# Two-layer transformer kernel: four blocks end, and three begin, by token tile over four steps

## The chip, the cores and the metric

The kernel runs on 1 core of one Trainium2 chip. The metric is device time in microseconds (us), the lower the better. TensorE (PE in the profile) multiplies, VectorE (DVE), ScalarE (ACT) and GpSimd (POOL) do the rest, and SyncE (SP) issues the transfers.

## What is computed

A first transformer layer (sliding-window attention beside a state-space mixer, then a gated MLP) is followed by a block of two more layers on 256 tokens of width 2048. The change lies in that block, whose core is:

```python
def rmsnorm(x, g):
    xf = x.astype(jnp.float32)
    y = xf * lax.rsqrt(jnp.mean(xf * xf, axis=-1, keepdims=True) + RMS_EPS)
    return (y * g.astype(jnp.float32)).astype(x.dtype)

def squared_relu_mlp(h, w_up, w_down):
    return jnp.square(jax.nn.relu(h @ w_up)) @ w_down

def second_block(x, ...):
    h = x
    for layer in range(DEPTH_2):
        hn = rmsnorm(h, norm_mix_pre[layer])
        if layer % 2 == 0:
            mix = gmlp_shortconv_mixer(hn, ...)      # ends in "@ w_out", 2048 x 2048
        else:
            mix = dilated_attention_mixer(hn, ...)   # begins with "@ w_qkv", ends in "@ w_o"
        h = h + rmsnorm(mix, norm_mix_post[layer])
        f = squared_relu_mlp(rmsnorm(h, norm_mlp_pre[layer]), w_up[layer], w_down[layer])
        h = h + rmsnorm(f, norm_mlp_post[layer])
    return h
```

Everything is float32. So at the end of each mixer and each MLP a 256 x 2048 result is normed (with the mean over all 2048 columns), added to h, and h, turned by TensorE, is the left operand of the next product.

## The kernel before

**Units and steps.** The program is a list of units (`Plan`). A unit is one product with up to 1024 output columns; it has 8 or 16 steps, one for each 128 rows of the weight. A step has two tile-steps, one for each tile of 128 tokens; in each, TensorE does six matmuls of 512 columns (`tile_step`, L2191): the left operand and the weight are each held as a high part and a rest, and high x HI, high x LO and rest x HI are summed, in two banks of PSUM. A step is so 12 matmuls.

**Splitting the weights.** SP loads two steps at a time into one of three buffers RAW. For each step ACT copies RAW to HI (`hi`, L659), rounded, and DVE subtracts to get LO (`lo`, L1251). The split of a step goes to one of four slots; `Plan.was` says which earlier step held the slot, and both engines wait for `step_done` of that step, which TensorE raises when it has done both its tile-steps. `split_by(i)` says up to which step can be split once all steps before i are done. Each engine's program is a fixed sequence, written out when the kernel is built, and each engine runs its own in order.

**The end of a block.** `post` (one on ACT, L1151, one on DVE, L1894) norms the result of a mixer or MLP. The blocks end with the units oab1 (mixer of layer 0), dn2.0.7.1 (its MLP), wo1.1 (mixer of layer 1) and dn2.1.7.1 (last MLP). In all four, both tiles of the last step come out of PSUM at its end, each by one instruction of 1024 columns (L1873, L1875) to ACC. ACT squares and sums them (L1136), DVE multiplies by the gain (L1885), adds the parts (L1900) and makes the mean (L1304), POOL makes the root for both tiles by a power (L2043), and DVE adds the product to XR, which is h, by 512 columns and tile (L1907, `x_added`). The products with the left half of the columns, and their squares and gains, are done during the last unit (`post_first`).

**The beginning of a block.** The units up2.0.0, qkv0.0 and up2.1.0 follow. Their left operand KPA is made in eight pairs of 128-column chunks by `feed`: TensorE transposes four 128 x 128 pieces of XR (L2248), ACT makes the high part (L706), DVE the rest (L1297). `due` says how many pairs must have been made ahead of a step. Here DVE makes the additions to XR for columns 512 to 2047 (`upto`); `squares` asks for all of them within the first steps. The sums of squares for the next norm (`squares`, ACT L719) are needed only when the unit's product leaves PSUM.

**Order by tile.** Ten units in `BY_TILE` end with their last two steps in another order: tile 0 of both, then tile 1 of both, and the unit after them begins likewise, so that tile 0 is out of PSUM one step earlier. The four units that end the blocks are not among them.

## Time and profile before

| | us |
|---|---|
| median of 3 runs | 3276.19 (3273.45 to 3278.97) |
| profiled execution, its own time | 3279.68 |
| its span in the profile | 3277.9 |
| TensorE busy in the span | 3221.9 (98%) |
| VectorE busy | 1867.7 (57%) |
| ScalarE busy | 1471.5 (45%) |
| DMA engines, mean busy share | 55% |

The span is the profiled execution as the trace has it; 1.8 us lie around it. "Busy" counts instructions on an engine, not waiting. The chain of waits is followed back from the last instruction, at each step to what released it: where it leaves TensorE, TensorE had nothing to do.

### The profile page before, as it was taken

Reading aid. Unit: us, or ns where it says so; the run is one execution under the profiler, and the core shown is the slowest. Engines: PE = TensorE matmul, PEld = TensorE weight load, DVE = VectorE, ACT = ScalarE, POOL = GpSimd, SP = SyncE. Lnnn points to the kernel's source line nnn. Section 1 sums busy time; section 2 is a strip of 40 time slices with the busy share of each in tenths; the row PEclk is TensorE's granted clock in tenths of the full one; section 3 lists DMA queues with packets and bytes.
Section 4 is the critical chain, followed back from the end, with each engine's and each line's share of the span. In section 5 each row is a group of like instructions: output and inputs, shape, how many; then the busy total and the mean of one; then the engine's idle time right before and its main releaser. Section 6 shows DMA issues by size and latency. Waiting matters only on the chain.

```text
span 3277.9 us, 38808 instructions
## 1 busy us (share of the span) xinstructions
PE 3221.9 (98%) x15914; PEld 2659.8 (81%) x15914; DVE 1867.7 (57%) x1979; ACT 1471.5 (45%) x1758; POOL 86.9 (3%) x80
## 2 busy tenths in 40 slices
PE   8999999999999999999999999999999999999998
PEld 6787888888888888878888888878887788888886
DVE  7676555555555645565555555565655655555555
ACT  7454544444444544454444444454444544444443
POOL 1120000000000000000000000010000000000000
PEclk9999999999999999999999999999999999999999
DMA  6344555555555555555555555545545455555554
GB/s 211 117 146 138 181 193 186 190 191 192 193 189 192 191 181 191 197 175 182 191 192 186 188 192 189 196 158 180 165 156 177 170 192 186 188 192 189 184 192 141
DMA packets 185516, 593.17 MB, mean 181 GB/s; under 512 B 12491, under 2 KB 17276, under 8 KB 184828
## 3 DMA queue, kind: packets, MB, share of 16 engines
q1 hardware_dynamic: 185340, 590.70, 55.0%
q8 instruction: 125, 2.05, 0.2%
q14 instruction: 51, 0.42, 0.0%
HBM read 588.54 MB, written 2.12 MB: 180 GB/s over the span
## 4 chain that ended last, share of the span: by engine, by line
PE 73%; issue 22%; DVE 3%; ACT 2%; DMA 0%; POOL 0%; SPq 0%; DVEq 0%; POOLq 0%; ACTq 0%
PE PS L2191 68%; PE PS L2248 1%; PE PS L2340 1%; DVE LO L1251 1%; PE PS L2212 1%; DVE XR L1907 0%; PE PS L2256 0%; ACT HI L659 0%; PE PS L2354 0%; PE PS L2360 0%; DVE KPA L1297 0%; DMA RAW<-in_w_in 0%; DVE ST L1595 0%; PE PS L2273 0%; ACT LG L935 0%
## 5 line engine op out<-in xcount | busy, mean ns | idle before, releaser
L1251 DVE TENSOR_TENSOR LO<-RAW,HI 128x1024 fp32r<-128x1024 f32 (+1 forms) x1104 | 1346.8, 1223 | 1103.8 <-ACT HI L659 1101.1
L659 ACT ACTIVATE HI<-RAW 128x1024 fp32r<-128x1024 f32 (+1 forms) x1104 | 1158.5, 1053 | 1312.6 <-PE PS L2191 1308.8
L2191 PE MATMUL PS<-HI,KPA 128*128 128x512 f32 x5312 | 1473.4, 394 | 5.4 <-ACT ACC L728 2.2
L2191 PEld LDWEIGHTS PS<-HI,KPA 128*128 128x128 f32 x5312 | 991.5, 189 | 213.0 <-issue 8.0
L2191 PE MATMUL PS<-HI,KPB 128*128 128x512 f32 x3392 | 935.3, 392 | 1.8 <-DVE ACC L1875 1.4
L2191 PE MATMUL PS<-LO,KPA 128*128 128x512 f32 x2656 | 827.1, 392 | 2.1 <-DVE LO L1251 1.1
L2191 PEld LDWEIGHTS PS<-HI,KPB 128*128 128x128 f32 x3392 | 631.1, 188 | 129.9 <-issue 1.8
L2191 PEld LDWEIGHTS PS<-LO,KPA 128*128 128x128 f32 x2656 | 500.3, 189 | 113.0 <-DVE LO L1251 4.7
L2191 PE MATMUL PS<-LO,KPB 128*128 128x512 f32 x1696 | 523.8, 390 | 0.0
L2191 PEld LDWEIGHTS PS<-LO,KPB 128*128 128x128 f32 x1696 | 318.7, 188 | 67.2
L701 ACT ACTIVATE KPB<-PS 128x512 fp32r<-128x512 f32 x98 | 58.5, 598 | 181.8 <-PE PS L2248 181.8
L1292 DVE TENSOR_TENSOR KPB<-PS,KPB 128x512 fp32r<-128x512 f32 x98 | 67.8, 692 | 120.7 <-ACT KPB L701 120.7
L2043 POOL TENSOR_TENSOR ST<-ST,NEG 128x2 f32<-128x2 f32 (+2 forms) x16 | 20.2, 1260 | 2794.2 <-DVE ST L1304 2793.9
L1873 DVE TENSOR_TENSOR ACC<-PS,ACC 128x1024 f32<-128x1024 f32 x60 | 70.8, 1218 | 10.0 <-PE PS L2191 9.6
L1297 DVE SCALAR_TENSOR_TENSOR KPA<-PS,PAR,KPA 128x256 fp32r<-128x256 f32 x96 | 42.0, 480 | 54.0 <-ACT KPA L706 53.8
L706 ACT ACTIVATE KPA<-PS,PAR 128x256 fp32r<-128x256 f32 x96 | 40.1, 469 | 57.9 <-PE PS L2248 57.4
L2248 PE MATMUL PS<-ID,XR 128*128 128x128 f32 x192 | 33.6, 300 | 23.0 <-DVE XR L1907 16.6
L1934 DVE TENSOR_TENSOR HS<-RL 128x1024 f32<-128x1024 f32 x32 | 39.2, 1226 | 24.3 <-ACT RL L1165 24.3
L2248 PEld LDWEIGHTS PS<-ID,XR 128*128 128x128 f32 x192 | 26.0, 154 | 31.8 <-DVE XR L1907 20.3
L2248 PEld LDWEIGHTS PS<-ID,HS 128*128 128x128 f32 x344 | 42.8, 140 | 11.0
L2248 PE MATMUL PS<-ID,HS 128*128 128x128 f32 x344 | 51.5, 272 | 0.0
L1165 ACT ACTIVATE RL<-PS,ST 128x1024 f32<-128x1024 f32 x32 | 35.8, 1119 | 26.6 <-DVE HS L1934 22.8
(272 smaller groups left out, 1022.9 us busy)
## 6 DMA issues: line engine op xcount, KB each, us to landing
RAW<-in_w_up SPq DMA_DIRECT2D x128, 1024.0 KB, 5.1
RAW<-in_w_down SPq DMA_DIRECT2D x128, 1024.0 KB, 5.5
RAW<-in_w_qkv SPq DMA_DIRECT2D x48, 1024.0 KB, 5.1
RAW<-in_w_ff_gate SPq DMA_DIRECT2D x88, 512.0 KB, 3.8
RAW<-in_w_ff_up SPq DMA_DIRECT2D x88, 512.0 KB, 4.7
RAW<-in_w_ff_down SPq DMA_DIRECT2D x44, 1024.0 KB, 5.5
RAW<-in_w_in_ab SPq DMA_DIRECT2D x40, 1024.0 KB, 5.0
RAW<-in_w_in SPq DMA_DIRECT2D x16, 1024.0 KB, 5.2
```

The costliest lines, as they stand in the source:

```text
L659: e.activation(HI[plan.slot[s]][:, 0:w], RAW[:, d % NRAW, j, 0:w], ACT.Copy).then_inc(S("hi_made"), 1)
L701: e.activation(kt[:, ks:ks + 2, 0, :], PS[:, bank, :].rearrange("p (a b) -> p a b", a=2), ACT.Copy).then_inc(S("chunk_hi"), 1)
L706: ins = e.activation(kt[:, ks + c, 0, :], PS[:, bank, c * 256:c * 256 + 256], ACT.Copy, scale=par(g.gain, 2 * j + c, 1))
L1165: e.activation(RL[:, :], flat2(b), ACT.Relu, scale=r[:, t:t + 1]).then_inc(S("evac_act"), 1)
L1251: e.tensor_tensor(LO[h][:, 0:w], RAW[:, d % NRAW, j, 0:w], HI[h][:, 0:w].bitcast(F32), ALU.subtract).then_inc(S("lo_made"), 1)
L1292: e.tensor_tensor(kt[:, ks:ks + 2, 1, :], PS[:, bank, :].rearrange("p (a b) -> p a b", a=2), kt[:, ks:ks + 2, 0, :].bitcast(F32), ALU.subt ...
L1297: ins = e.scalar_tensor_tensor(out=kt[:, ks + c, 1, :], in0=PS[:, bank, c * 256:c * 256 + 256], scalar=par(g.gain, 2 * j + c, 1), in1=kt[: ...
L1873: ins = e.tensor_tensor(d, flat2(b), d, ALU.add)
L1934: e.tensor_tensor(HS[b % 2][:, t, :], RL[:, :], RL[:, :], ALU.mult).then_inc(S("squared_relu"), 1)
L2191: ins = e.matmul(PS[:, b + j, 0:cw], l, r[h][:, 512 * j:512 * j + cw], start=(i == 0 and part == 0), stop=(last and part == 2))
L2212: ins = e.matmul(PS[:, f // 2, 256 * (f % 2):256 * (f % 2) + 256], l[h][:, w], kt[:, ks, r, :], start=(i == 0 and part == 0 and f % 2 == 0 ...
L2248: ins = e.transpose(PS[:, bank, c * 256 + t * 128:c * 256 + t * 128 + 128], src(2 * j + c, t), ID[:, :])
```

## The change

1. The four last units of the blocks are by tile over their last four steps (tile 0 of all four, then tile 1 of all four), and the units after them over their first four. TensorE's transposes of the first four chunks of XR are made for tile 0 ahead of the last tile-step of tile 1 in the old unit, and for tile 1 ahead of the last tile-step of tile 0 in the new one.
2. Two more slots for splits, HI5/LO5 and HI6/LO6, from the first step of each of these last units to the sixth step of the unit after it. The slots have 1024 columns each and lie where activations of other stages lie.
3. The right half of the result leaves PSUM, and is squared and multiplied by the gain, in halves of 512 columns; mean and root are made for each tile by itself.
4. The steps at which pairs are made are three tables (`NORM_DUE`, `NORM_DUE_PE`, `NORM_DUE_DVE`); the additions to XR for columns 512 to 2047 are made only as `feed` comes to them; the squares of XR are put off by 7 steps on ACT, the mean by 9 on DVE.
5. SP writes the output of tile 0 first, then tile 1; the load of the rope table waits at step 12 of qkv0.0 and not at step 8.

```diff
@@ class Plan: make_steps, make_slots, done
-            u.closes, u.opens = u.name in BY_TILE, n > 0 and self.units[n - 1].name in BY_TILE
+            u.closes, u.opens = BY_TILE.get(u.name, 0), BY_TILE.get(self.units[n - 1].name, 0) if n else 0
...
+        more = {self.by_name[n].first: n for n in BY_TILE if BY_TILE[n] == 4}
+        fewer = [self.units[self.by_name[n].number + 1].first + 6 for n in BY_TILE if BY_TILE[n] == 4
+                 and self.by_name[n].number + 1 < len(self.units)]
...
+            if s in more:
+                used[5], used[6] = -2, -1
+                self.taken[s] = self.taken[s + 1] = more[s]
+            if s in fewer:
+                del used[5], used[6]
...
-            self.was.append(used[h])
+            self.was.append(max(used[h], -1) if h > 4 else used[h])
...
+    def done(self, u, i):
+        if i < u.opens:
+            return u.first + max(0, 2 * i - u.opens)
+        return u.first + i
...
-BY_TILE = ("ws0", "ws1", "qkv0.0", "qkv0.1", "qkv0.2", "qkv1.0", "qkv1.1", "qkv1.2", "wo0.0", "wo0.1")
+BY_TILE = {n: 2 for n in ("ws0", "ws1", "qkv0.0", "qkv0.1", "qkv0.2", "qkv1.0", "qkv1.1", "qkv1.2", "wo0.0", "wo0.1")}
+BY_TILE |= {n: 4 for n in ("oab1", "dn2.0.7.1", "wo1.1", "dn2.1.7.1")}
+NORM_DUE = (1, 2, 2, 3, 4, 5, 5, 6, 6, 7, 7, 8, 8, 8, 8, 8)
+NORM_DUE_PE = (2, 2, 2, 3, 4, 5, 5, 6, 6, 7, 7, 8, 8, 8, 8, 8)
+NORM_DUE_DVE = (2, 2, 2, 3, 4, 5, 5, 6, 6, 7, 7, 8, 8, 8, 8, 8)
...
@@ ScalarE: post
+        def post(name, first, last, feeder=None):
+            pn, u = PN[name], U[last]
+            unit(last, None, [post_first(name, first)])
             for t in range(2):
-                post_square(name, 1, t, second)
+                for c in (2, 3):
+                    q.wait_ge(S("post_squared"), pn["squared"] + 2 * t + c)
+                    if c == 2:
+                        q.wait_ge(S("half_out"), pn["added"] // 4 + t + 1)
+                    else:
+                        q.wait_ge(S("evac_dve"), u.ed[t])
+                    k = 2 * (c - 1) + t
+                    e.activation(JK[:, 0:512], ACC[:, t, 512 * c:512 * c + 512], ACT.Square,
+                                 accum_out=pn["part"][:, k:k + 1]).then_inc(S("post_squared"), 1)
+                if t == 0:
+                    hi(plan.split_by(u.last - 1))
+                    if feeder is not None:
+                        next(feeder)
...
@@ VectorE: unit, squares, post
-                if not (hold and i == u.nk - 1 or u.closes and i == u.nk - 1 and evac is not None):
-                    lo(plan.split_by(u.first + i - (u.opens and i == 1)))
+                if u.closes == 4 and i >= u.nk - 2 or u.closes == 2 and i == u.nk - 1 and evac is not None:
+                    pass
+                elif i < u.opens == 4:
+                    if i >= 2:
+                        lo(u.first + i + 2)
+                else:
+                    lo(plan.split_by(plan.done(u, i)))
...
-        def squares(name, before=None):
+        def squares(name):
             nm = NM[name]
             for c in range(2):
-                if before is not None:
-                    before(2 * c + 1)
...
+        def post(name, last, before=None, following=None):
+            pn, u = PN[name], U[last]
+            unit(last, None, [post_first(name)])
+            first_gained = gained.n
+            ready = {}
+            def out(t, c):
+                d, ps = ACC[:, t, 512 * c:512 * c + 512], PS[:, u.bank[t] + c - 2, :]
+                if before is not None:
+                    q.wait_ge(S("evac_dve"), U[before].ed[t])
+                    ins = e.tensor_tensor(d, ps, d, ALU.add)
+                else:
+                    ins = e.tensor_copy(d, ps)
+                if c == 2:
+                    halves(ins)
+                else:
+                    ins.then_inc(S("evac_dve"), 1)
+            def half_gain(t, c):
+                if c == 2:
+                    q.wait_ge(S("half_out"), halves.n)
+                else:
+                    q.wait_ge(S("evac_dve"), u.ed[t])
+                ready[t, c] = gain(name, t, 512 * c, 512 * c + 512, 2 * t + c + 1)
...
-                q.wait_ge(S("root_made"), ROOT[name])
-                q.wait_ge(S("gained"), n if c < 2 or t == 0 else n + 1)
+                q.wait_ge(S("root_made"), ROOT[f"{name}.{t}"])
+                q.wait_ge(S("gained"), first_gained if c < 2 else ready[t, c])
...
+            feeder = feed(following, before=upto) if following else None
+            for t in range(2):
+                q.wait_ge(S("tile0_done") if t == 0 else S("step_done"), u.number + 1 if t == 0 else u.last + 1)
+                out(t, 2)
+                out(t, 3)
+                half_gain(t, 2)
+                mean_of(t)
+                if feeder is None:
+                    half_gain(t, 3)
+                    for c in range(4):
+                        add(c, t)
+                elif t == 0:
+                    half_gain(t, 3)
+                    add(0, t)
+                    lo(u.last + 3)
+                    next(feeder)
+                else:
+                    lo(u.last + 4)
+                    add(0, t)
+                    half_gain(t, 3)
+            return feeder
@@ VectorE: ffn2
+                        unit(f"up2.{layer}.{b}", nf, [late(ms, 9)], [ms], evac, have=1, ahead=NORM_DUE_DVE)
...
@@ TensorE: matmuls, tile_step, unit, ffn2
-                if u.opens and i < 2:
-                    tile_step(u, n, i)
-                elif u.closes and i >= u.nk - 2:
-                    tile_step(u, u.nk - 2 + n, i - (u.nk - 2))
+                if i < u.opens:
+                    tile_step(u, (2 * i + n) % u.opens, (2 * i + n) // u.opens)
+                elif i >= u.nk - u.closes:
+                    k = 2 * (i - u.nk + u.closes) + n
+                    tile_step(u, u.nk - u.closes + k % u.closes, k // u.closes)
                 else:
...
+            made = g.first + (t if g.by_tile and i < 4 else i // 2) + 1
...
-                    q.wait_ge(S("chunk_lo"), g.first + i // 2 + 1)
+                elif part == 2:
+                    q.wait_ge(S("chunk_lo"), made)
...
+                     lambda i, between: matmuls(u, i, last_mid if between is None else between), have, mids)
...
+                if g.by_tile and j < 2:
+                    for c in range(4):
+                        ready(c, j)
+                        ins = e.transpose(PS[:, bank, c * 128:c * 128 + 128], src(c, j), ID[:, :])
...
+                        unit(f"up2.{layer}.{b}", nf, mids=[second(nf)], have=2, ahead=NORM_DUE_PE)
...
@@ SyncE
-            if d == dma_of("qkv0.0", 8):
+            if d == dma_of("qkv0.0", 12):
```

**DVE at the end of oab1.** The names: LO5_81 and LO6_83 are the new slots, LO4_79 the fourth slot, LO_53 the first three; ACC is the block's result, ST small statistics, GPM the gain, KPA the next unit's left operand. Before, the last splits in front of the result are of steps whose slots are free; the result leaves PSUM in pieces of 1024 columns:

```order
L1251 TENSOR_TENSOR LO4_79<-RAW_51,HI4_78 128x1024 [waits step_done,hi_made]
L1251 TENSOR_TENSOR LO_53<-RAW_51,HI_52 128x1024 [waits step_done,hi_made] x2
L1875 COPY ACC_54<-PS 128x1024 [waits tile0_done]
L1875 COPY ACC_54<-PS 128x1024 [waits step_done]
L1885 TENSOR_TENSOR ACC_54<-ACC_54,GPM_118 128x1024 [waits post_squared]
L1900 TENSOR_TENSOR ST_57<-ST_57 128x2 [waits post_squared]
L1304 TENSOR_SCALAR ST_57<-ST_57 128x2 [waits dve_own]
L1907 SCALAR_TENSOR_TENSOR XR_49<-ACC_54,ST_57,XR_49 128x512 [waits gained,root_made]
L1907 SCALAR_TENSOR_TENSOR XR_49<-ACC_54,ST_57,XR_49 128x512
```

After, in the same place:

```order
L1314 TENSOR_TENSOR LO4_79<-RAW_51,HI4_78 128x1024 [waits step_done,hi_made]
L1314 TENSOR_TENSOR LO5_81<-RAW_51,HI5_80 128x1024 [waits step_done,hi_made]
L1997 COPY ACC_54<-PS 128x512 [waits tile0_done]
L1997 COPY ACC_54<-PS 128x512
L1974 TENSOR_TENSOR ACC_54<-ACC_54,GPM_122 128x512 [waits post_squared,half_out]
L2013 TENSOR_TENSOR ST_57<-ST_57 128x1
L2014 TENSOR_SCALAR ST_57<-ST_57 128x1 [waits dve_own]
L2016 SCALAR_TENSOR_TENSOR ST_57<-ST_57 128x1 [waits post_squared,dve_own]
L1974 TENSOR_TENSOR ACC_54<-ACC_54,GPM_122 128x512 [waits evac_dve]
L2023 SCALAR_TENSOR_TENSOR XR_49<-ACC_54,ST_57,XR_49 128x512 [waits gained,root_made]
L1375 SCALAR_TENSOR_TENSOR KPA_50<-PS,PAR_55,KPA_50 128x128 [waits chunk_hi,turned]
L1375 SCALAR_TENSOR_TENSOR KPA_50<-PS,PAR_55,KPA_50 128x128 x3
```

What moved: the split into LO5_81 (step 2 of the next unit) now stands ahead of the first piece of tile 0, and it waits for `step_done` of oab1's fourth step from the end. The first addition to XR for tile 0 stands ahead of all that is done for tile 1, whose pieces follow in the same pattern.

**DVE in the first steps of qkv0.0**, from the rest of the third pair on. Before:

```order
L1297 SCALAR_TENSOR_TENSOR KPA_50<-PS,PAR_55,KPA_50 128x256 [waits chunk_hi,turned]
L1297 SCALAR_TENSOR_TENSOR KPA_50<-PS,PAR_55,KPA_50 128x256
L1251 TENSOR_TENSOR LO_53<-RAW_51,HI_52 128x1024 [waits step_done,hi_made]
L1297 SCALAR_TENSOR_TENSOR KPA_50<-PS,PAR_55,KPA_50 128x256 [waits chunk_hi,turned]
L1297 SCALAR_TENSOR_TENSOR KPA_50<-PS,PAR_55,KPA_50 128x256
L1251 TENSOR_TENSOR LO_53<-RAW_51,HI_52 128x1024 [waits step_done,hi_made]
L1907 SCALAR_TENSOR_TENSOR XR_49<-ACC_54,ST_57,XR_49 128x512
L1907 SCALAR_TENSOR_TENSOR XR_49<-ACC_54,ST_57,XR_49 128x512 [waits gained]
L1907 SCALAR_TENSOR_TENSOR XR_49<-ACC_54,ST_57,XR_49 128x512 x2
```

After:

```order
L1385 SCALAR_TENSOR_TENSOR KPA_50<-PS,PAR_55,KPA_50 128x256 [waits chunk_hi,turned]
L1385 SCALAR_TENSOR_TENSOR KPA_50<-PS,PAR_55,KPA_50 128x256
L1314 TENSOR_TENSOR LO6_83<-RAW_51,HI6_82 128x1024 [waits hi_made]
L1385 SCALAR_TENSOR_TENSOR KPA_50<-PS,PAR_55,KPA_50 128x256 [waits chunk_hi,turned]
L1385 SCALAR_TENSOR_TENSOR KPA_50<-PS,PAR_55,KPA_50 128x256
L1314 TENSOR_TENSOR LO_53<-RAW_51,HI_52 128x1024 [waits step_done,hi_made] x3
L1314 TENSOR_TENSOR LO4_79<-RAW_51,HI4_78 128x1024 [waits step_done,hi_made]
L2023 SCALAR_TENSOR_TENSOR XR_49<-ACC_54,ST_57,XR_49 128x512 [waits gained] x2
L1385 SCALAR_TENSOR_TENSOR KPA_50<-PS,PAR_55,KPA_50 128x256 [waits chunk_hi,turned]
L1385 SCALAR_TENSOR_TENSOR KPA_50<-PS,PAR_55,KPA_50 128x256
```

What moved: the additions of columns 1024 to 1535 stood behind one split after the fourth pair, with those of columns 1536 to 2047 right behind; they now stand behind four splits (behind two of them in up2.0.0), and those of columns 1536 to 2047 later still.

**PE at the end of oab1.** HI5_80, HI6_82 and so on are the slots; KPB is oab1's left operand. Before, the transposes of XR stand behind the last matmul of oab1:

```order
L2191 MATMUL PS<-LO4_79,KPB_69 128x512
L2191 MATMUL PS<-HI4_78,KPB_69 128x512 x4
L2191 MATMUL PS<-LO4_79,KPB_69 128x512 x2
L2191 MATMUL PS<-HI4_78,KPB_69 128x512 x2
L2248 MATMUL PS<-ID_56,XR_49 128x128 [waits x_added] x2
L2248 MATMUL PS<-ID_56,XR_49 128x128 x6
L2191 MATMUL PS<-HI_52,KPA_50 128x512 [waits evac_dve,chunk_hi,hi_made]
```

After:

```order
L2330 MATMUL PS<-HI_52,KPB_69 128x512 x2
L2330 MATMUL PS<-LO_53,KPB_69 128x512 x2
L2330 MATMUL PS<-HI_52,KPB_69 128x512 x2
L2388 MATMUL PS<-ID_56,XR_49 128x128 [waits x_added]
L2388 MATMUL PS<-ID_56,XR_49 128x128 x3
L2330 MATMUL PS<-HI_52,KPB_69 128x512 x2
L2330 MATMUL PS<-LO_53,KPB_69 128x512 x2
L2330 MATMUL PS<-HI_52,KPB_69 128x512 x2
L2330 MATMUL PS<-HI_52,KPA_50 128x512 [waits evac_dve,chunk_hi,hi_made]
L2330 MATMUL PS<-HI_52,KPA_50 128x512
L2330 MATMUL PS<-LO_53,KPA_50 128x512 [waits lo_made]
```

What moved: four transposes (tile 0) wait for `x_added` while the last tile-step of tile 1 still stands behind them. Four more (tile 1) stand likewise ahead of the last tile-step of tile 0 in up2.0.0.

## Rows read from the trace of the kernel before

**Rows 1.** The page: busy time of each engine.
```profile
PE 3221.9 (98%) x15914; PEld 2659.8 (81%) x15914; DVE 1867.7 (57%) x1979; ACT 1471.5 (45%) x1758; POOL 86.9 (3%) x80
```
**Rows 2.** Waits of PE over the span: total us, times, longest.
```profile
PE PS L2248 <- DVE XR L1907: 16.6, 11, 4.8
```
**Rows 3.** Chain from 1380 on, oab1 to up2.0.0: start us, us, what.
```profile
1379.90 24.49 PE PS L2191 x108
...
1404.42 1.23 DVE ACC L1875
...
1416.91 0.55 PE PS L2248 x3
1417.46 2.78 PE PS L2191 x12
1420.24 0.44 PE PS L2248 x4
```
**Rows 4.** The same chain, dn2.0.7.1 to qkv0.0.
```profile
2114.82 14.07 PE PS L2191 x62
...
2141.68 0.55 PE PS L2248 x3
2142.23 2.75 PE PS L2191 x12
```
**Rows 5.** The same chain, wo1.1 to up2.1.0.
```profile
2535.83 3.87 PE PS L2191 x17
...
2552.23 0.55 PE PS L2248 x3
2552.78 2.76 PE PS L2191 x12
```
**Rows 6.** Timeline of qkv0.0 about its fourth pair: start us, us, engine, instruction.
```profile
2144.82 0.60 PE L2248 MATMUL PS<-ID,XR 128*128 128x128 f32 x4
...
2145.46 0.84 ACT L706 ACTIVATE KPA<-PS,PAR 128x256 fp32r<-128x256 f32 x2 [0.37 <-PE PS L2248]
...
2146.40 0.88 DVE L1297 SCALAR_TENSOR_TENSOR KPA<-PS,PAR,KPA 128x256 fp32r<-128x256 f32 x2 [1.09 <-ACT KPA L706]
```
**Rows 7.** The page's groups: count, busy us, mean ns of one.
```profile
L1251 DVE TENSOR_TENSOR LO<-RAW,HI 128x1024 fp32r<-128x1024 f32 (+1 forms) x1104 | 1346.8, 1223 | 1103.8 <-ACT HI L659 1101.1
L659 ACT ACTIVATE HI<-RAW 128x1024 fp32r<-128x1024 f32 (+1 forms) x1104 | 1158.5, 1053 | 1312.6 <-PE PS L2191 1308.8
L701 ACT ACTIVATE KPB<-PS 128x512 fp32r<-128x512 f32 x98 | 58.5, 598 | 181.8 <-PE PS L2248 181.8
L1292 DVE TENSOR_TENSOR KPB<-PS,KPB 128x512 fp32r<-128x512 f32 x98 | 67.8, 692 | 120.7 <-ACT KPB L701 120.7
```
**Rows 8.** Groups by form, whole span: smaller shapes and the sums.
```profile
L1629 DVE TENSOR_TENSOR q_sb<-PS,ST 128x128 f32<-128x128 f32 x16 | 3.9, 286 | 6.0 <-PE PS L2439 5.9
L1907 DVE SCALAR_TENSOR_TENSOR XR<-ACC,ST,XR 128x512 f32<-128x512 f32 x32 | 22.2, 748 | 3.2 <-POOL ST L2043 3.2
L719 ACT ACTIVATE JK<-XR 128x1024 f32<-128x1024 f32 x24 | 25.2, 1051 | 16.3 <-DVE XR L1907 16.3
```
**Rows 9.** Timeline at the end of the program: start us, us, engine, instruction.
```profile
3263.31 0.61 PE L2191 MATMUL PS<-HI,KPB 128*128 128x512 f32 x2
...
3266.46 0.16 DVE L1900 TENSOR_TENSOR ST<-ST 128x2 f32<-128x2 f32 x1
...
3266.91 0.70 POOL L2043 TENSOR_TENSOR ST<-ST,NEG 128x2 f32<-128x2 f32 x1 [697.79 <-DVE ST L1304]
...
3270.10 4.06 DVE L1907 SCALAR_TENSOR_TENSOR XR<-ACC,ST,XR 128x512 f32<-128x512 f32 x6
```
**Rows 10.** PE in windows of 1 us after a short stall: length, busy, granted clock.
```profile
247.00:248.00 1.00, 0.16 (x2) 1.00 0.91 311
...
250.00:251.00 1.00, 1.00 (x4) 0.50 0.04 16
```
**Rows 11.** The same after the long stall behind oab1.
```profile
1412.00:1413.00 1.00, 1.00 (x3) 0.50 0.00 0
```

More of the change, by code:

```diff
@@ L311, in first_half, with second @@
         yield
+def second(g):
+    yield
+    next(g)
+    yield
 def often(g):
@@ L1910, in post @@
-            add(0, 1)
-            gain(name, 1, 1)
             made = [0]
@@ L2703, in tensor @@
             else:
-                unit("qkv0.0", norm("pre1", added(PN["mlp0"]["added"])))
+                unit("qkv0.0", nf_pre1, mids=[second(nf_pre1)], have=2, ahead=NORM_DUE_PE)
             gq = turn8(hf, 0, "q")
@@ L2715, in tensor @@
         drain(old)
-        for c in range(2):
-            unit(f"wo1.{c}")
-        ffn2(1, norm("mpre1", added(PN["mix1"]["added"])))
+        unit("wo1.0")
+        unit("wo1.1", last_mid=lambda: next(nf_mpre1))
+        ffn2(1, nf_mpre1, None)
     with nc.Block() as block:
```

185 lines of the change are left out of this document (115 added, 70 removed).

## The prediction, made blind

> **What bounds the kernel now.** I read the page first: TensorE is busy for 3221.9 of 3277.9 us [rows 1], so whatever is gained or lost lies in its 56 us of waiting. The table of waits names the largest of these: transposes of XR that wait for DVE's additions, 16.6 us in 11 waits [rows 2]. The chain of waits shows what each block end costs in full. From oab1's last matmul (1379.90 + 24.49 = 1404.4) to 1417.46, where TensorE goes on without a stop, there are 13.06 us; in them it does one step, 12 matmuls in 2.75 us, and three pairs of transposes, 0.44 us each, together 4.07. So 9.0 us are lost [rows 3]. Behind dn2.0.7.1 it is 2142.23 - 2128.89 = 13.34, lost 9.3 [rows 4]; behind wo1.1 2552.78 - 2539.70 = 13.08, lost 9.0 [rows 5]. Together **27.3 us**. After the very last matmul the chain to the last addition takes 10.2 us (3263.92 to 3274.16) [rows 9], and 3.7 more to the end of the span.
>
> **Method.** The engines run fixed sequences, so I laid the new sequences out with the durations of the rows. Zero is the start of the last four steps of an old unit. A tile-step is half of 2.75, 1.37 us. HI is 1.05, LO 1.2 [rows 7]. A half out of PSUM or times the gain is 0.67, between half of 1.223 and 0.692 [rows 7]. A half square with its sum is 0.70: 0.598 [rows 7] and what of the read shows behind it. The three small DVE instructions of a mean are 0.19 each, as 0.16 with its gap, the root 0.70 [rows 9]. An addition is 0.70, from 4.06 for six to 0.748 alone [rows 8, 9]. The high part of a 128x128 piece is no row: between half (0.21) and all (0.42) of the 0.42 that one of two takes [rows 6], I take 0.31, and for DVE 0.29, near the 0.286 of another 128x128 [rows 8].
>
> **What it removes.** All three gaps above, and in exchange each wait that the new sequence has. Nothing is removed from TensorE's own work: as many matmuls and as many transposes.
>
> **Wait 1, tile 0's transposes, 3.9 us.** Tile 0 is out at 4 tile-steps, 5.5. But DVE stands at the split for slot LO5 first, whose slot comes free with the fourth last step, now done after five tile-steps, 6.85. HI ends at 7.95, LO at 9.2. Two halves out: 10.55. Square of the second half: 11.3; mean 11.9, root 12.7, addition 13.4. TensorE reaches the transposes after seven tile-steps, at 9.6, with the last tile-step of the old unit queued behind them: it waits 3.9. Without the split in front, the addition would end at 9.8 and the wait would be 0.2.
>
> **Wait 2, tile 1's transposes, 1.4 us**, and 0.8 of small ones. The old unit ends at 15.3. DVE makes the rests of tile 0 until 16.6 (four high parts, four rests behind the transposes, which cost TensorE 0.4 at the first tile-step), then two halves out 17.9, gain 18.7, mean 19.2, a split 20.4 (the root ends beside it, at 20.0), addition 21.1. TensorE is there at 19.8. Tile 1's high parts and rests cost 0.4 again.
>
> **Wait 3, third pair, 0.8 us.** Behind tile 1's rests stand a split and two additions: 1.2 + 1.4 against two tile-steps.
>
> **Wait 4, fifth pair, 3.1 us in up2.0.0 and 5.5 us in the other two.** This one can be read from the trace nearly whole. From the start of the fourth pair's transposes to the end of DVE's rests are 2147.28 - 2144.82 = 2.46 us [rows 6]. Then the change puts two or four splits (2.4 or 4.8) and two additions (1.4): 6.3 or 8.7 with the semaphores. TensorE has 0.44 and one step, 3.2 us, before it asks for the fifth pair. Before, one split stood there and the pair was asked for no earlier.
>
> **Wait 5, seventh pair, 1.5 us.** The additions of columns 1536 to 2047 now follow the split of step 11, which waits for step 7. From the sixth pair on: high parts 0.84, HI 1.05, a square of XR with its sum 1.2, HI 1.05, LO 1.2, additions 1.4, and semaphores, against 0.44 and two steps [rows 6 to 8].
>
> Sum at oab1: 3.9 + 1.4 + 0.8 + 0.8 + 3.1 + 1.5 = 11.5; at the other two 13.9. Together **39.3, against 27.3: +12.0 us**.
>
> **The clock.** After the long stall behind oab1 the granted clock is 0.50 of full, the 1.2 GHz level, still at 1412, under matmuls [rows 11]. That cost nothing before, because the way ran through DVE's splits and additions. But the granted clock also falls after a stall of 1.8 us (TensorE idle in most of 247 to 248, clock 0.50 at 250 with TensorE fully busy [rows 10]). The new stalls are 3.9, 3.1 or 5.5, and 1.5 us, and behind the last two lies nothing but matmuls. The low stretches last 3.3 to 6.6 us; where TensorE is busy through one, half of it is lost, 1.7 to 3.3. Wait 2 covers most of what follows wait 1. I take 0.7 + 2 per block end, **+8 us** in all, with 0 and 15 as ends.
>
> The Trainium skill ("TensorE: Matmul & The Clock Gate", section "Why this matters for your kernels") names long idle gaps between bursts of matmuls as what brings TensorE down to its lower clock. Read so, only wait 4 in qkv0.0 and up2.1.0, as long as the stall behind oab1, would surely count, and the term would be 2 x 2 = 4 us. The row at 250 shows a fall after a shorter stall, so the trace goes further than the page, and I keep 8.
>
> **The end of the program, -3.2 us.** Tile 0's norm runs beside tile 1's four tile-steps: tile 0's last addition ends 0.8 us behind the last matmul. Then two halves out 1.35, squares until 2.9, mean 3.5, root 4.2, four additions 7.0. Before it was 10.2. The transfer behind the last addition stays, 3.7. Ends: -2.6 to -3.6.
>
> **Moved things at no cost.** SP's load of the next gain stands behind the eighth addition, now some 7 steps later, and in front of the weights of steps 14 and 15. The addition ends 1.1 + 1.2 + 1.6 = 4 us into step 8; gain and weights, 1 MB each, would be there some 9 us later, near the end of step 12: two steps to spare. If that cover were gone, a step would wait for its transfer, and ACT and DVE would stand behind it. The mean of the next norm moves to step 13 of 16; its root has two steps. Two slots more ask DVE for two splits earlier in an 8-step unit, 2.4 us of which it has 1.5 a step.
>
> **Sum**: 12.0 + 8 - 3.2 = +16.8 us. Against the profiled execution's own 3279.68 that is 3296. That execution lies 3.5 above the median of the runs, 3276.19; for the median I say **3292**, a little under 3293.
>
> **Rivals.** *A, faster: the tile order hides the norm as drawn.* If DVE's split ahead of tile 0 did not bind (for instance because its slot is free by the time DVE is there) and the fifth pair's additions were in time, waits 1 and 4 vanish: 39.3 - 11.7 - 14.1 = 13.5, against 27.3, and -3.2: -17, time 3259. It decides at the point where the fourth last step is done before tile 0 is. For it: DVE is busy only 57% [rows 1]. Against it: both waits are in the written sequence. 14%. *B, about the same:* one of the waits is shorter than I lay it out, by about 4 us at each end, and the clock stays up: 12.0 - 12 - 3.2 = -3, 3273. 17%. *C, slower without the clock:* 12.0 - 3.2 = +8.8, time 3285. 27%. *D, the change does not do what it says*, the slots or the order unused: the sequences show both, 2%, within B. **My forecast**, with the clock's part: 40%.
>
> **How the numbers follow.** A change of 0.2%, 6.6 us, is about what a measurement of this kernel can tell from none. The forecast and C are slower, 67%; B and D about the same, 19%, and A, 14%, faster. The unknown costs: small pieces at all of the 0.42 add 2 us a block end, at half take 1 away; clock 0 to 15; end of program 1. So the forecast's own range is 3281 to 3304. To hold 8 in 10 I take in C and most of B: **3274 to 3305**; left out are A and the far end.
>
> **What would show it.** Right: in the chain or the waits, transposes of XR waiting about 3.9 us with oab1's last tile-step still to come; the same line waiting about 3 us in up2.0.0 and 5.5 us in qkv0.0 and up2.1.0, four splits deep; windows of granted clock 0.5 under matmuls behind them; last matmul to last addition 7.0. Wrong: DVE's first half-copy starting right at `tile0_done`, the fifth pair without a wait, or less than 27 us lost over the three block ends.

## The result: 0.5% slower, and where the time stands in the profile after

The changed kernel takes **3293.48 us** (median of 4 runs, 3291.76 to 3295.59) against 3275.83 of the kernel before beside it; the ratio is **1.0051**, with a 95% interval of 1.0039 to 1.0063. The profiled execution took 3293.84 us with a span of 3291.7, so 13.8 us more span than before.

The page of the changed kernel, busy time by engine, and two rows of its table of waits (engine, line, what is waited for: total us, times, longest); they answer to [rows 1] and [rows 2]:

```profile
PE 3227.2 (98%) x15914; PEld 2660.5 (81%) x15914; DVE 1870.2 (57%) x2023; ACT 1473.7 (45%) x1786; POOL 90.2 (3%) x84
```
```profile
PE PS L2388 <- DVE XR L2023: 14.6, 6, 4.2
PE PS L2392 <- DVE XR L2023: 14.4, 15, 4.4
```

L2388 transposes the first two pairs, tile by tile, L2392 the later ones. Together TensorE waits 29.0 us for additions to XR, where it waited 16.6, and 21 times where it waited 11 times. At each block end there are now five places to wait; they are called wait 1 to wait 5, as in the prediction. The chain at the first block end, with its columns start us, us, what, answers to [rows 3]:

```profile
1400.24 1.07 ACT HI L688
...
1401.33 1.23 DVE LO L1314
1402.56 0.61 DVE ACC L1997
...
1405.30 0.94 POOL ST L2179
...
1406.27 0.76 DVE XR L2023
...
1407.08 1.11 PE PS L2388 x4
```

Tile 0 was complete before all this (TensorE is three tile-steps further at 1402.86, so near 1398.7, by an estimate from 1.37 us each), yet the first copy out of PSUM (L1997) starts only at 1402.56, behind ACT's rounding and DVE's split of a weight tile that has nothing to do with it. The second large wait is the fifth pair's. DVE's and PE's timelines at the second block end (start us, us, instruction, [idle before <-releaser]):

```profile
2155.46 4.62 DVE L1314 TENSOR_TENSOR LO<-RAW,HI 128x1024 fp32r<-128x1024 f32 x4
2159.99 1.41 DVE L2023 SCALAR_TENSOR_TENSOR XR<-ACC,ST,XR 128x512 f32<-128x512 f32 x2
```
```profile
2160.80 0.33 PE L2392 MATMUL PS<-ID,XR 128*128 128x128 f32 x1 [4.36 <-DVE XR L2023]
2161.46 0.90 PE L2392 MATMUL PS<-ID,XR 128*128 128x128 f32 x3 [0.34 <-DVE XR L2023]
```

Four splits, 4.62 us, stand ahead of the two additions on which TensorE waits 4.7 us in all. After both large waits the granted clock is at half. Windows of PE (length, busy of PE, weight loads, DVE, ACT, POOL, then granted clock, DMA share, GB/s); the last one, behind a wait of 0.7 us, is at full clock:

```profile
1407.00:1408.00 1.00, 0.92 (x5) 0.92 (x6) 0.03 (x1) 0.00 (x0) 0.00 (x0) 0.50 0.00 0
...
1420.00:1421.00 1.00, 1.00 (x6) 0.66 (x4) 1.00 (x2) 0.00 (x0) 0.00 (x0) 1.00 0.00 0
1432.00:1433.00 1.00, 1.00 (x4) 0.75 (x3) 0.62 (x2) 1.00 (x2) 0.00 (x0) 0.50 0.98 406
1446.00:1447.00 1.00, 1.00 (x6) 0.81 (x5) 0.31 (x1) 1.00 (x3) 0.00 (x0) 1.00 0.94 246
```

The three block ends lie in the windows 1380:1460, 2100:2190 and 2505:2605. Over these the table has TensorE's idle time and its loss to the half clock (busy time times one less the granted clock). The third column counts from one matmul ahead of each end to the same matmul behind it, and says how much longer the three ends take than in the kernel before; each profile has the same 15914 TensorE records, ewarm 40 more of its own, left out here. The fourth is how many stretches at half clock (3.4 us each at 0.50, so at most 1.7 us lost) each profile has **elsewhere**, ahead of the last unit:

| kernel | idle, three ends | lost to the clock there | three ends, against before | stretches elsewhere | span |
|---|---|---|---|---|---|
| before | 16.9 | 7.9 | 0 | 4 | 3277.9 |
| changed | 29.2 | 9.9 | +17.0 | 4 | 3291.7 |
| after2 (changed, again) | 29.1 | 12.2 | +19.1 | 2 | 3291.2 |
| e1 | 20.7 | 6.9 | +6.9 | 2 | 3278.3 |
| e2 | 15.0 | 5.1 | -4.7 | 2 | 3267.3 |
| eb | 25.1 | 9.2 | +12.5 | 1 | 3283.0 |
| e3 | 6.4 | 0.0 | -16.8 | 0 | 3251.5 |
| e4 | 5.0 | 0.0 | -17.7 | 0 | 3250.5 |
| e5 | 2.5 | 0.0 | -20.7 | 0 | 3247.5 |
| ewarm | 20.6 | 5.7 | +13.7 | 1 | 3283.1 |

From before to changed the ends are 17.0 us longer (4.7, 6.1 and 6.2): 12.2 idle, 2.0 clock and 2.8 that are neither. The end of the program gives 3.2 back: from the last matmul to the end of the span it took 14.0 us and takes 10.8, of which the additions make 2.6 and the transfer behind them 0.6. That is the span's 13.8. The 2.8 are short: a pair whose pieces come one by one takes 0.33 + 0.55 us of transposes where it took 0.44, and the first two matmuls behind a wait take 0.70 instead of 0.61. The first two columns are a count and not a price: a TensorE that comes late to a wait, because it was slow, waits less there.

### The profile page after: what moved, and what is told of

Read it like the earlier page. It is cut to its first block, busy times and chain, and to the rows that moved or that the text cites. A ratio compares the mean times of both kernels' runs of the same rounds, so it can differ in the third digit from the quotient of the medians.

```text
span 3291.7 us, 38854 instructions
## 1 busy us (share of the span) xinstructions
PE 3227.2 (98%) x15914; PEld 2660.5 (81%) x15914; DVE 1870.2 (57%) x2023; ACT 1473.7 (45%) x1786; POOL 90.2 (3%) x84
## 4 chain that ended last, share of the span: by engine, by line
PE 94%; DVE 3%; ACT 2%; issue 1%; POOL 0%; DMA 0%; DVEq 0%; POOLq 0%; SPq 0%; ACTq 0%
PE PS L2330 87%; PE PS L2392 2%; DVE LO L1314 1%; PE PS L2484 1%; PE PS L2351 1%; DVE XR L2023 1%; ACT HI L688 1%; PE PS L2400 0%; PE PS L2498 0%; POOL ST L2179 0%; PE PS L2504 0%; PE PS L2417 0%; ACT LG L982 0%; PE PS L2623 0%; DVE ST L1681 0%
## 5 line engine op out<-in xcount | busy, mean ns | idle before, releaser
L2179 POOL TENSOR_TENSOR ST<-ST,NEG 128x2 f32<-128x2 f32 (+3 forms) x20 | 23.7, 1183 | 2831.7 <-DVE ST L2016 1786.0
L1959 DVE TENSOR_TENSOR ACC<-PS,ACC 128x1024 f32<-128x1024 f32 x54 | 63.5, 1218 | 0.0
L2392 PEld LDWEIGHTS PS<-ID,HS 128*128 128x128 f32 x344 | 42.6, 140 | 11.2
L2392 PE MATMUL PS<-ID,HS 128*128 128x128 f32 x344 | 51.5, 272 | 0.0
L2392 PE MATMUL PS<-ID,XR 128*128 128x128 f32 x168 | 29.5, 292 | 20.8 <-DVE XR L2023 14.4
L2392 PEld LDWEIGHTS PS<-ID,XR 128*128 128x128 f32 x168 | 21.5, 147 | 30.1 <-DVE XR L2023 19.0
```

What stands on the lines that cost most here:

```text
L1959: ins = e.tensor_tensor(d, flat2(b), d, ALU.add)
L2392: ins = e.transpose(PS[:, bank, c * 256 + t * 128:c * 256 + t * 128 + 128], src(2 * j + c, t), ID[:, :])
```

## Experiments

All are timed beside the kernel before on the same chip, in three groups, in which that kernel had medians of 3275.79 (e1, e2, e3, eb), 3278.34 (e4, etail, ewarm) and 3278.68 (e5, after2, etail2); across groups I compare ratios and traces, not medians.

### e1: the split ahead of tile 0's copies

```
-  if not (u.closes == 4 and i >= u.nk - 2 or ...):     # ACT; DVE alike
+  if not (u.closes == 4 and i >= u.nk - 3 or ...):
```

> Edit: at the closing steps of a unit that ends by token tile, ACT's and VectorE's splits for the third-last step's successor two on (step +2 of the next unit) are held until tile 0's chain is through, as those behind them already are. Everything else is the changed kernel. Theory (the first wait, 4.2 us in the trace of the changed kernel at each of the three block ends, is the wait of VectorE's split for a weight slot that TensorE frees only at the fourth-last tile-step's end, and tile 0's evacuation stands behind that split): the wait before tile 0's transposes falls from 4.2 to 1 us or less, the wait before tile 1's grows by about 1, and the first of the two stretches at half clock (3.4 us, some 1.7 us of time) goes at each end; 2.5 to 4.2 us an end, 3281 to 3286 us in all, against 3293.5. Rival 1 (tile 0's wait is the length of its own chain, rest, root and scale, 1.4 + 0.8 + 0.9 + 0.8 us, whatever stands in the queue): first wait still 3 us or more, 3291 to 3294. Rival 2 (the held splits come too late for step +2): the first wait goes, but a new wait for the right operand KPR appears at step +2, 3292 to 3297.

Measured: **3279.08 us**, ratio 1.0008 (0.9999 to 1.0016), 14 us less than the changed kernel. Waits of e1 over the span, and the second wait of the first end:

```profile
PE PS L2392 <- DVE XR L2023: 14.3, 15, 4.4
...
PE PS L2388 <- DVE XR L2023: 6.3, 6, 1.5
```
```profile
1410.00 0.66 PE L2388 MATMUL PS<-ID,XR 128*128 128x128 f32 x4 [1.53 <-DVE XR L2023]
```

The first wait went from 4.2 to 0.57 at each end, the second rose to 1.5, the later ones are untouched. So tile 0's wait was the place of one split in two queues. The median fell by 14, more than the theory's 7.5 to 12.6, but the three ends are 10.1 us shorter, inside it; the rest of the span, 3.3, goes with two stretches elsewhere less. The first stretch at half clock is gone at each end, but behind the fourth wait it is twice as long, 6.8 us, in the second and third end of this profile. The held splits came late for nobody (rival 2): no wait for a split appears at step +2.

### e2: the additions behind the splits

```
-  if before is not None and j % 2 == 0:
-      before(j // 2)
+  if before is not None:
+      before(min((j + 1) // 2, 3))
```

> Edit: in VectorE's order in a unit that begins by token tile, the additions that a tile waits for stand ahead of the rests of the odd pair too (before: only ahead of the even pair's), so that the additions of a tile are one pair earlier in the queue. Nothing else differs from the changed kernel. Theory (waits 3, 4 and 5, measured at 0.2 / 2.4 / 0.7 us in the first end and 0.2 / 4.6 / 0.7 in the other two, come of the additions standing behind VectorE's splits of the step that is next in the queue): these waits fall to under 0.5 us each, the second stretch at half clock (some 1.7 us) goes at each end, 5.0 / 7.3 / 7.2 us, 3274 us in all (3272 to 3278), about the kernel before. Rival (the additions wait for TensorE's tile or for POOL's rests rather than for their place in the queue): waits stay over 2 us, 3288 to 3294.

Measured: **3267.72 us**, ratio 0.9977 (0.9968 to 0.9986). This one edit turns the change from a loss into a gain. The whole of its waits for XR:

```profile
PE PS L2388 <- DVE XR L2023: 14.9, 6, 4.2
```

L2392's row is gone: waits 3, 4 and 5 all vanish, not only fall, and with them the second stretch at half clock at each end. Expected were 19.5 us; the three ends are 21.7 shorter: 14.1 idle, 4.8 clock, and the 2.8 of short pieces, which went with the waits. The median fell by 25.8; 2.8 of the span's 24.4 go with two stretches elsewhere, which nothing ties to this edit.

### eb: two splits or four

```
+  elif i == u.opens == 4:
+      lo(u.first + 7)
```

> Edit: in the units that begin by token tile, VectorE's splits of the first opening step reach only to step +7, so that two splits and not four stand ahead of the additions on which the fifth pair's transposes wait in the second and third block end (two stand there in the first). Theory (a wait of 2.4 us behind two splits and of 4.7 and 4.5 us behind four: the splits' number sets the wait): the second and third wait fall to about 2.4 us, 4.5 us less in all, 3289 us (3288 to 3290). Rival (the wait is set by TensorE's slots, so that the splits that remain wait as long): 3293 to 3294, waits of 4.5 us as before.

Measured: 3284.44 us, ratio 1.0026 (1.0016 to 1.0036). The waits in the windows of the second and third end read the same (lines moved by two):

```profile
PE PS L2394 <- DVE XR L2025: 3.3, 5, 2.1
```

They were 5.6 and 5.5 in the changed kernel; the fifth pair's is 2.4 of it instead of 4.7 and 4.5, as in the first end. The price of 1.15 us for one split in the queue is thus read directly: the wait falls by 2.3 for two. The three ends are 4.5 us shorter, as the waits say, of the 9 us between the medians. The rest goes with three stretches elsewhere that this profile does not have, 4.2 us of its span. The rival is out, but the total alone would have misled by a factor of two. One more thing shows here: of the three waits of 2.4 us that this profile has, the first and third are followed by a stretch at half clock, the second is not.

### e3: both queue edits

> Edit: the two edits of e1 and e2 together (held splits at the end of the block, additions one pair earlier at its beginning). Theory (both causes are separate places of VectorE's queue and their prices add): 12 less 19.5 taken together give 27 to 32 us less than the changed kernel, 3261 to 3267 us, which is 9 to 15 us less than the kernel before. Rival (what e1 and e2 take away comes back at the next operation, since VectorE has the same work to do in the 29 us of the two units): the two prices overlap and the sum is no better than the better one of the two, 3274 to 3280.

Measured: **3255.38 us**, ratio 0.9940 (0.9926 to 0.9953): 38 us below the changed kernel, where e1 and e2 alone gave 14 and 26. At the three ends alone it is 33.8 us, where e1 and e2 gave 10.1 and 21.7: the prices add, with 2 us more, and no stretch at half clock is left there. The expected 27 to 32 was passed by the median also because this profile has none of the four stretches elsewhere, 6.3 us of its span. Wide windows of the changed kernel, then of e3 (columns as above):

```profile
100.00:300.00 200.00, 194.36 (x2185) 160.54 (x2184) 132.19 (x248) 91.93 (x178) 39.15 (x39) 0.97 0.43 131
1380.00:1460.00 80.00, 71.32 (x309) 56.84 (x308) 44.35 (x65) 35.59 (x58) 2.53 (x3) 0.96 0.44 152
```
```profile
100.00:300.00 200.00, 193.54 (x2207) 160.42 (x2206) 135.80 (x253) 94.10 (x182) 39.16 (x39) 1.00 0.43 132
1380.00:1460.00 80.00, 77.86 (x357) 62.89 (x356) 50.57 (x72) 41.66 (x64) 3.12 (x3) 1.00 0.51 173
```

The second row of each is the block end: 8.7 us idle became 2.1, and the clock stays at full. The first row is a stretch that the edits do not touch: three stretches at half clock there in the one execution and none in the other. The spans of e3's five executions tell the same: 3251.5, 3251.5, 3253.2, 3253.2 and 3256.5, in steps near 1.7 or a multiple, with mean clocks from 0.999 to 0.997. So such stretches come in some executions only, and put up to 5 us of scatter on them; where they lay in the executions that were not profiled, no trace tells.

### e4: POOL's root and its neighbour on DVE

What remained in e3 was 0.57 and 1.5 us per end. DVE's and POOL's timelines of e3 at tile 1:

```profile
1404.29 0.16 DVE L2016 SCALAR_TENSOR_TENSOR ST<-ST 128x1 f32<-128x1 f32 x1
1404.37 1.22 DVE L1314 TENSOR_TENSOR LO<-RAW,HI 128x1024 fp32r<-128x1024 f32 x1
1406.04 0.75 DVE L2023 SCALAR_TENSOR_TENSOR XR<-ACC,ST,XR 128x512 f32<-128x512 f32 x1 [0.45 <-POOL ST L2179]
```
```profile
1396.95 0.94 POOL L2179 TENSOR_TENSOR ST<-ST,NEG 128x1 f32<-128x1 f32 x1 [256.42 <-DVE ST L2016]
1404.53 1.47 POOL L2179 TENSOR_TENSOR ST<-ST,NEG 128x1 f32<-128x1 f32 x1 [6.64 <-DVE ST L2016]
```

The root of one column takes 1.47 us beside a split of 1.22 and ends 0.41 after it (1406.00 against 1405.59); in tile 0 it takes 0.94 beside a gain of 0.69.

```
   elif t == 0:
-      half_gain(t, 3)
       add(0, t)
+      half_gain(t, 3)
   ...
   else:
-      lo(u.last + 4)
       add(0, t)
+      lo(u.last + 4)
```

> Edit: on top of e3 (both queue edits), VectorE's additions of the first 512 columns stand directly behind the mean of their tile at each block end, ahead of the second half's gain (tile 0) and of a weight split (tile 1). So VectorE issues nothing while POOL takes the root. The end of the program is left as it is. Theory (in e3 POOL's root of one column takes 0.94 us in tile 0 and 1.47 in tile 1, and each time it ends 0.41 to 0.42 us after the end of the VectorE operation that started beside it, a gain multiplication of 0.69 us and a split of 1.22: POOL's operation waits for that one; with nothing beside it the root of two columns took 0.69 us in the kernel before): both roots take about 0.69 us, the wait before tile 0's transposes falls from 0.57 to about 0.3 us, that before tile 1's from 1.5 to about 0.75, 1.0 us an end, 3 us in all, 3252 us against 3255.4. Rival (the root's length is POOL's own, whatever runs beside it; a profile's POOL spans are rough): roots of 0.94 and 1.47 as before, and the split that now stands behind comes 1.5 us later, 3255 to 3258.

Measured: 3256.09 us, ratio 0.9932 (0.9919 to 0.9944), not to be told from e3 by its time. The trace tells: POOL's two roots of e4, and its waits at the first end:

```profile
1396.80 0.56 POOL L2179 TENSOR_TENSOR ST<-ST,NEG 128x1 f32<-128x1 f32 x1 [256.42 <-DVE ST L2016]
1404.01 0.56 POOL L2179 TENSOR_TENSOR ST<-ST,NEG 128x1 f32<-128x1 f32 x1 [6.65 <-DVE ST L2016]
```
```profile
PE PS L2330 <- DVE KPA L1375: 0.8, 1, 0.8
PE PS L2388 <- DVE XR L2023: 0.8, 2, 0.6
```

Both roots take 0.56 us once DVE issues nothing beside them, 0.9 less for tile 1. So the theory's mechanism holds and the rival is out. The waits for XR fell by 1.3 an end, but a new one of 0.85 stands behind: the rests of tile 1 come late, and of the 3 us only 1 is left in the span. The Trainium skill ("SBUF — State Buffer", section "Who interferes with whom") says that a VectorE instruction with two inputs in SBUF, as gain and split are, contends with a GpSimd instruction that reads SBUF, and that issue order decides who blocks. The trace agrees: gain and split were issued first, and the root took 0.94 and 1.47 us beside them, 0.56 alone.

The kernel before had the same effect in sight, though not at the place of [rows 9]: its roots for the norm ahead of the next product, of two columns too, stand beside a split and take 1.61 us where those of the block ends take 0.70.

```profile
1432.04 1.23 DVE L1251 TENSOR_TENSOR LO<-RAW,HI 128x1024 fp32r<-128x1024 f32 x1
1432.20 1.61 POOL L2043 TENSOR_TENSOR ST<-ST,NEG 128x2 f32<-128x2 f32 x1 [24.15 <-DVE ST L1304]
```

### e5: the rests of tile 1 ahead of the additions

```
-  if before is not None:
+  if before is not None and j != 1:
       before(min((j + 1) // 2, 3))
   ...                                   # behind the rests of the pair
+  if before is not None and j == 1:
+      before(1)
   ...                                   # upto(c): tile 1's second gain moves in
+  if made[0] == 1:
+      half_gain(1, 3)
```

> Edit: on top of e4, VectorE's gain of tile 1's second half and its additions of the second 512 columns stand behind the rests of tile 1's first eight pieces instead of ahead of them. Theory (in e4 the two waits for the transposes fell to 0.19 and 0.60 us, but a new one of 0.85 us stands behind them, TensorE's for VectorE's rest of tile 1, which starts only after split, gain and two additions, 1.22 + 0.68 + 1.41 us, though ScalarE's rounding was ready 1.1 us earlier): this wait goes, or falls under 0.1, 0.8 us an end, 2.5 us in all, 3253.6 us and a span of 3248 in the profile. Rival (the additions then come too late for the third pair's transposes): a wait of 0.5 us or more there, 3255 to 3256 as e4.

Measured: **3250.55 us**, ratio **0.9917** (0.9903 to 0.9930), 28 us less than the kernel before. The wait of 0.85 is gone and no new one stands there: the idle time of the three ends is 2.5 us, nearly all of it the 0.19 and 0.62 us ahead of the two tiles' transposes. The span of 3247.5 is the expected 3248; the median is 3 us below the 3253.6, which was named from e4's median, 5.6 above e4's span. Against the kernel before, 20.7 us of the span's 30.4 stand at the three ends and 3.2 at the end of the program; 6.4 go with the four stretches elsewhere, which no edit here is shown to remove. This is the fastest version, and it is the change as it was made with five places in DVE's order (one of them in ACT's too) moved.

### ewarm: what the clock costs

```
+  if g.by_tile and j == 4:
+      for _ in range(WARM_N[name]):             # 8, 16, 16
+          e.matmul(PS[:, 0, 0:512], KPA[:, 0, 0, 0:128], KPA[:, 0:2, 0, :], start=True, stop=True)
```

> Edit: in the changed kernel, ahead of the transposes of the fifth pair of each of the three norms, TensorE runs 8, 16 and 16 matmuls of 512 columns on operands that lie ready, into a bank that nobody reads; they fill the fourth wait (2.4, 4.7 and 4.7 us) and add nothing to the output. Theory (after that wait the granted clock stands at 0.50, 1.2 instead of 2.4 GHz, for 3.4 us, in which busy TensorE loses 1.7 us): the half-clock stretches behind the fourth wait are gone, those behind the first stay, 5.1 us less than the changed kernel, 3288.4 us. Rival (the stretch at half clock costs nothing, because the engines behind it set the pace then, or it comes all the same): 3293 to 3294; with the extra matmuls overrunning the wait, up to 3297.

Measured: 3286.86 us, ratio 1.0026 (1.0017 to 1.0035); by ratios 8 us less than the changed kernel's 1.0051, and 6 less than after2's 1.0044, in another group each, so the size is rough. Expected were 5.1. Timeline of ewarm at the third end and a window behind the second:

```profile
2565.93 3.79 PE L2388 MATMUL PS<-KPA 128*128 128x512 f32 x16
2570.45 0.33 PE L2396 MATMUL PS<-ID,XR 128*128 128x128 f32 x1 [0.73 <-DVE XR L2024]
```
```profile
2156.00:2157.00 1.00, 0.60 (x3) 0.41 (x4) 0.68 (x2) 0.00 (x0) 0.00 (x0) 1.00 0.99 401
```

With work that nobody needs in the gap, the granted clock behind the fourth wait stays at 1.00, and TensorE's loss to the clock at the three ends falls from 9.9 to 5.7. The three ends are 3.3 us shorter than the changed kernel's, less than the 5.1: in the third one the stretch behind wait 1 is twice as long, 6.8 us, in this profile. The other 5.3 us of the span's 8.6 go with three stretches elsewhere, so the median's fall is not the price. That the stretch behind wait 4 is a cost of its own, on top of the wait that brings it, is shown; its size, by the first two ends, is 1.6 and 1.1 us.

### etail, after2, etail2: the end of the program

```
-BY_TILE |= {n: 4 for n in ("oab1", "dn2.0.7.1", "wo1.1", "dn2.1.7.1")}
+BY_TILE |= {n: 4 for n in ("oab1", "dn2.0.7.1", "wo1.1")}
```

> Edit: the last unit of the program is taken out of the list of units that end by token tile, so that it ends as in the kernel before (both tiles' last steps together); the three block ends stay as in the changed kernel. Theory (the part of the change at the end of the program gains what the traces say, 10.2 less 7.6 us from the last matmul to the last addition, and perhaps a little by the matmuls of tile 1 running on while tile 0 is normed): 2.6 to 4 us more than the changed kernel, 3296 to 3297.5 us, 11 to 12 us from the last matmul to the last addition, since the halves and one root per tile add instructions to the chain. Rival (the output's transfer hides the additions, so the end by tile gains nothing): 3293 to 3294.

> The changed kernel itself, unedited, on the same chip and beside the same runs of the kernel before as the next one. Theory and rival both expect 3293 to 3296; its spread tells what the waits elsewhere in the program (stretches at half clock of 1.7 us that are in some executions and not in others) do to a median.

> The kernel of etail again (the program's end not by token tile), beside the changed kernel on the same chip. In etail the stretch from the last matmul to the last addition went from 7.6 to 11.7 us, 4.1 more, but the median stood only 1.8 us above the changed kernel's of another chip. Theory (4.1 us on the path that ends the program; the rest of the difference was chance in the half-clock stretches elsewhere): 3 to 5 us above the changed kernel of this group. Rival (matmuls in the last steps run earlier when both tiles end together, so that the end by tile gains under 1 us): within 1 us of it.

Measured: etail 3295.32 us, ratio 1.0054 (1.0040 to 1.0068), between what theory and rival named, which told nothing beside the changed kernel of another group. After2, the changed kernel again: 3292.80 us (3289.22 to 3295.63), just under the 3293 to 3296 named, ratio 1.0044 (1.0032 to 1.0057). Etail2 beside it: 3296.68 us, ratio 1.0055 (1.0041 to 1.0069), **3.9 us more**, though the ranges of the two overlap. The last matmul and last additions of the changed kernel, then of etail:

```profile
3280.32 0.61 PE L2330 MATMUL PS<-HI,KPB 128*128 128x512 f32 x2
```
```profile
3281.98 1.28 DVE L1995 TENSOR_TENSOR ACC<-PS,ACC 128x512 f32<-128x512 f32 x2
...
3285.78 2.74 DVE L2023 SCALAR_TENSOR_TENSOR XR<-ACC,ST,XR 128x512 f32<-128x512 f32 x4 [0.44 <-POOL ST L2179]
```
```profile
3275.43 0.61 PE L2330 MATMUL PS<-HI,KPB 128*128 128x512 f32 x2
```
```profile
3284.97 2.74 DVE L2023 SCALAR_TENSOR_TENSOR XR<-ACC,ST,XR 128x512 f32<-128x512 f32 x4 [0.44 <-POOL ST L2179]
```

From the last matmul's end to the last addition's: 7.6 us (3280.93 to 3288.52) against 11.7 (3276.04 to 3287.71). The end by tile is thus worth 4.1 us given the halves, which themselves had cost 1.5 (11.7 against the 10.2 of before).

## Why the prediction was right, and where its steps were not

The forecast was 3292 with 3274 to 3305, the result 3293.48. Direction, mechanism and size hold; the terms were off by more than their sum, since they missed in both directions:

| term | forecast | measured |
|---|---|---|
| wait 1 | 3.9 each | 4.2 each |
| wait 2 | 1.4 | 1.1, 0.4, 0.5 behind half clock; 1.5 at full clock |
| wait 3 | 0.8 | 0.2 to 0.3 |
| wait 4 | 3.1, 5.5, 5.5 | 2.4, 4.7, 4.5 |
| wait 5 | 1.5 | 0.7 |
| waits in all, at full clock | 36.9 | 31.8 (estimate: 29.2 idle and the 2.6 that wait 2 was cut by) |
| small waits, short pieces, restarts | 2.4 | 5.2 |
| clock | 8 | 7.3 (estimate: 9.9 less the same 2.6) |
| less what the ends lost before | 27.3 | 27.3 |
| three ends | +20.0 | +17.0 |
| end of program | -3.2 | -3.2 |
| span | +16.8 | +13.8 |

**Wait 1** is right in mechanism and size, and e1 shows it. The 0.3 that it is longer is mostly the root, 0.94 instead of the 0.70 taken from [rows 9], where DVE stood idle.

**Wait 2** was laid out at full clock: 1.4. In e1, where no half-clock stretch precedes it, it is 1.5. In the changed kernel it was 1.1, 0.4 and 0.5, since TensorE was slow behind wait 1 and came later: what the clock takes ahead of a wait, the wait gives back in part, 2.6 us in all.

**Waits 3 to 5** are what the text says, additions queued behind splits (e2 removes all, eb half of the largest), but each was 0.5 to 0.8 us too long, and this is the term that was most mis-sized: 21.0 us forecast, 14.4 measured. For wait 4 the chain at the first end gives the reason: from the fourth pair's transposes to the end of its rests 2.30 us instead of 2.46, two splits 2.27 instead of 2.4, two additions 1.33 instead of 1.4; and the first transpose runs between the two additions, 0.33 us that are not waiting. For wait 5 the pieces that the text lists add up to 6.7 us against 5.9, which is 0.8; the other 0.7 was put down to semaphores, and is not in the trace. For wait 3 it lists 2.6 against two tile-steps, 2.7, which is no wait at all, and yet says 0.8.

**The clock** was near in size, 7.3 for 8. Behind wait 4 the stretch costs its full price, for wait 5 is 0.7 with it and without (ewarm). The text says that the half clock behind oab1's stall cost nothing in the kernel before, because the way ran through DVE. Busy at 0.50, TensorE lost 2.0, 3.2 and 2.7 us there, but the chain, here at the first end, nearly bears the text out:

```profile
1409.56 0.92 PE PS L2248 x3
...
1413.17 2.36 DVE LO L1251 x2
1415.53 1.34 DVE XR L1907 x2
```

Behind these additions TensorE waited at all three ends, so most of what the clock took there, the wait gave back. Only the three transposes of the first line, 0.92 us where three take 0.55 at full clock [rows 3], lay on the way: 0.4 us an end, 1.1 in all, as an estimate. So the two sums of the table of kernels, 7.9 and 9.9, must not be subtracted to get the price of the clock; by these estimates it went from 1.1 to 7.3. No run holds the old kernel's clock up, so the 1.1 is argued from its chain.

The rule of the Trainium skill that was weighed there ("TensorE: Matmul & The Clock Gate", section "Why this matters for your kernels"), that long idle gaps bring TensorE to its lower clock, with wait 4 in two ends alone as its price, would have given 4. The trace has a fall behind waits of 4.2, of 4.7 and also of 2.4 us, and none behind one of 0.7, so falls came after more of the waits than that reading allowed.

**The end of the program**: tile 0's additions end 1.1 us behind the last matmul (0.8 forecast), and the root took 0.93 beside a gain, so the last addition ends 7.6 us behind it, not 7.0. The transfer behind it, 3.7 us and said to stay, took 3.2.

**Luck** is in how near the median came. The ends grew by 3.0 us less than forecast, but the profiled execution of the kernel before, 3279.68, lies 3.9 above the median of the runs beside the changed kernel, and the changed kernel's, 3293.84, only 0.4 above its own: the medians differ by 17.7, the spans by 13.8.

**Rivals.** A, the order hides the norm, was held off by exactly the two places that the text named as its condition: with the split moved (e1) and the additions in time (e2), e3 gives 3255, and A had said 3259. B wanted shorter waits and the clock up; the windows at 0.50 exclude it. C, without the clock, named 3285; against it stands ewarm, whose three ends are 3.3 us shorter with the fourth wait filled and the second fall of the clock gone. D is excluded by the chain, in which the new order stands.

## What to carry to other kernels

When a norm is cut by tile to run beside matmuls, the work that must come first is not late because the engine is full (DVE is 57% busy) but because of what stands ahead of it in that engine's own order: here one split ahead of the first copy and two to four ahead of an addition cost 34 us at the three ends, and moving them turned 0.5% slower into 0.6% faster (e3), with three smaller moves 0.8% (e5). Read for each wait what its releaser did in the microseconds before, and whether TensorE needed that by then. A stretch at half clock costs its full price only where nothing but TensorE's own work follows; ahead of a wait for another engine the wait gives part or most of it back. So ask of each stretch which engine the chain goes through behind it, before and after the change. And a median can hold more than the edit: look in the profile for what changed far from it.

## What the runs showed of the hardware

- Each fall of the granted clock lasted about 3.4 us at 0.50, or twice that: at most 1.7 us of work lost for each 3.4. At the block ends of the changed kernel and its edits a fall stood behind all 31 waits of 4.2 to 4.7 us (six of them of double length), behind six of eight waits of 2.4 us (not at eb's second end and etail2's first), and behind none of the six of 1.5 us (e1, e3) or those of 0.7. Behind the old kernel's stalls of 4.5 to 4.8 us it was of double length at all three ends. So the ends vary too: 9.9 and 12.2 us lost in two executions of the changed kernel.
- Elsewhere a profile has 0 to 4 such stretches, and they change between executions of the same kernel. Behind the stall of 1.8 us near 246 one stands in four of twelve profiles. The one near 127 has no stall of 0.1 us within 30 us before it: it begins under 64 small matmuls, with which TensorE is busy throughout (the kernel before, columns as above):

```profile
123.46 3.85 PE L2340 MATMUL PS<-ACC,BLT 32*128 32x64 f32 x64
126.00:127.00 1.00, 1.00 (x18) 1.00 (x16) 0.50 (x1) 0.00 (x0) 0.00 (x0) 0.73 0.00 0
```

- This is a scatter of some 1.7 us steps, and a limit to what medians tell of edits worth 3 us. Waits that no half-clock stretch precedes repeated within 0.1 us.
- POOL's root of one column takes 0.56 us alone and ends 0.41 us after a VectorE operation with two operands in SBUF that runs beside it, 0.94 to 1.47 us in all; one of two columns takes 0.70 alone and 1.61 beside a split.
- Why all four stretches elsewhere (near 127, 250, 287 and 2480 us) are absent from the profiles of e3, e4 and e5 was not tested. Three of them lie ahead of everything that the edits touch; chance would do, but that is only argued.
